# Attention steps on TensorE: the dense unit's hi and lo products around the turned weights, and exponentials ahead of the copy on ScalarE

## What is computed

```
p = h @ w_in[l]                                   # dense: GLU, q/k/v, gates
u = a * sigmoid(g); u = dwconv1d(u, dw, dw_b)     # convolution branch, 31 taps
u = silu(layernorm(u, ln_g, ln_b))
q, k = rope_2d(q), rope_2d(k)
s = concat([q . k_window + bias, q . k_context])  # 8 heads of 64
p = softmax(s)
out = p_window @ v_window + p_context @ v_context
y = sigmoid(gates) * (conv, attention branches)
```

## Time and profile before

| what | value |
|---|---|
| median of 3 runs | 3333.02 us (3327.91 to 3340.66) |
| profiled execution | 3339.16 us, span of the core 3336.9 us |
| PE, PEld busy | 87%, 71% |
| DVE, ACT, POOL busy | 53%, 37%, 46% |
| mean granted clock of TensorE | 0.932 of full |
| POOL `split_lo`, line 223 | 493 x 2482 ns |
| ACT `split_hi`, line 215 | 493 x 1054 ns |
| DVE taps, line 1834 | 234 x 1232 ns |

### The profile page before, as it was taken

How to read it: one execution, slowest core, us unless ns; L and a number is a source line. 1 busy time by engine, 2 the same in 40 slices (tenths; PEclk the granted TensorE clock), 3 DMA queues, 4 the chain that set the end, 5 groups by cost and what they waited for, 6 DMA issues and landing times.

```text
span 3336.9 us, 44321 instructions
## 1 busy us (share of the span) xinstructions
PE 2909.7 (87%) x15992; PEld 2353.6 (71%) x15992; DVE 1755.2 (53%) x2143; ACT 1234.8 (37%) x1781; POOL 1534.0 (46%) x773
## 2 busy tenths in 40 slices
PE   6988788999999775789789878999979887899997
PEld 6977434777777765689667666787767666677876
DVE  6866663352334556645478745423334985452424
ACT  4443222332233343454424432523332363243423
POOL 3442201333444585567477623444445773334443
PEclk9978899999999898899899998999989998999999
DMA  4302796222332322355332112222232221223221
GB/s 174 99 29 77 228 323 218 88 71 81 101 94 86 104 89 94 104 157 163 102 98 72 59 57 76 95 94 90 94 106 82 76 64 57 76 76 100 93 91 69
DMA packets 125811, 342.47 MB, mean 103 GB/s; under 512 B 37216, under 2 KB 45536, under 8 KB 125024
## 3 DMA queue, kind: packets, MB, share of 16 engines
q1 hardware_dynamic: 96800, 321.71, 29.7%
q10 hardware_dynamic: 28864, 18.76, 2.0%
HBM read 330.61 MB, written 7.45 MB: 101 GB/s over the span
## 4 chain that ended last, share of the span: by engine, by line
PE 57%; DVE 14%; POOL 7%; issue 6%; DVEq 5%; ACT 4%; DMA 3%; POOLq 2%; ACTq 1%; SPq 0%
PE ps L258 28%; PE ps L276 18%; POOL wlo L223 7%; DVE co L1834 4%; DVEq L1835 3%; DMA wraw<-w_ada 2%; PE ps L1942 2%; POOLq L1925 2%; DVE nacc L350 1%; ACT whi L215 1%; PE ps L565 1%; DVE sm L1810 1%; DVE mv L1996 1%; PE ps L1564 1%; DVE pex L1819 1%
## 5 line engine op out<-in xcount | busy, mean ns | idle before, releaser
L223 POOL TENSOR_TENSOR wlo<-wraw,whi 128x1024 fp32r<-128x1024 f32 x493 | 1216.2, 2482 | 1686.2 <-ACT whi L215 1685.4
L215 ACT ACTIVATE whi<-wraw 128x1024 fp32r<-128x1024 f32 x493 | 518.0, 1054 | 643.3 <-PE ps L276 286.9
L258 PE MATMUL ps<-xhi,whi 128*128 128x512 f32 (+2 forms) x1728 | 569.6, 352 | 8.9 <-DVE fa L2053 5.0
L258 PE MATMUL ps<-xlo,whi 128*128 128x512 f32 (+2 forms) x1728 | 565.1, 349 | 0.0
L258 PE MATMUL ps<-xhi,wlo 128*128 128x512 f32 (+2 forms) x1728 | 354.7, 349 | 5.9 <-POOL wlo L223 5.9
L258 PEld LDWEIGHTS ps<-xhi,whi 128*128 128x128 f32 x1728 | 318.8, 190 | 57.8 <-issue 7.5
L258 PEld LDWEIGHTS ps<-xlo,whi 128*128 128x128 f32 x1728 | 318.7, 190 | 44.9 <-issue 1.0
L258 PEld LDWEIGHTS ps<-xhi,wlo 128*128 128x128 f32 x1728 | 282.6, 189 | 50.2 <-POOL wlo L223 6.5
L1834 DVE SCALAR_TENSOR_TENSOR co<-ub,vec,co 128x512 f32<-128x512 f32 (+1 forms) x234 | 279.2, 1232 | 6.4 <-issue 0.9
L258 PE MATMUL ps<-hhi,whi 128*128 128x512 f32 (+1 forms) x616 | 223.1, 369 | 5.6 <-DVE gt L1993 3.3
L258 PE MATMUL ps<-hlo,whi 128*128 128x512 f32 (+1 forms) x616 | 222.4, 368 | 0.0
(11 more groups left out here) (322 smaller groups left out, 5016.6 us busy)
## 6 DMA issues: line engine op xcount, KB each, us to landing
wraw<-stream SPq DMA_DIRECT2D x493, 512.0 KB, 3.4
wraw<-w_ada SPq DMA_DIRECT2D x96, 512.0 KB, 5.6
biasb<-attn_bias ACTq DMA_DIRECT2D x32, 256.0 KB, 3.5
xin<-x0T SPq DMA_DIRECT2D x4, 528.0 KB, 6.3
s_u<-uk ACTq DMA_DIRECT2D x8, 264.0 KB, 2.9
res<-x0T ACTq DMA_DIRECT2D x1, 2048.0 KB, 8.7
s_y<-yk ACTq DMA_DIRECT2D x64, 32.0 KB, 4.0
yf<-s_y SPq DMA_DIRECT2D x8, 256.0 KB, 2.9
```

What stands on the lines that cost most here:

```text
L215: act.activation(whi[:, s], wraw[:, s], ACT.Copy).then_inc(hi_done[s], 1)
L223: pool.tensor_tensor(wlo[:, s], wraw[:, s], whi[:, s].bitcast(F32), ALU.subtract).then_inc(lo_done[s], 1)
L258: last = pe.matmul(ps[:, bank, 0:b - a], w[:, s, kt], x[:, kt, c0 + a:c0 + b], start=start, stop=stop)
```

## The change

In `mix_pe`, `pe_filler` is cut in two: `pe_filler_hi` issues the hi products, `pe_filler_lo` the lo products. In a step the turn of the step before stands between the hi and the lo products of the step's last unit; the values stand at the end of the step, behind the unit and its post product. Behind the last step of scores this holds too: the turn of step N - 1 stands between hi and lo of unit U+28, the values of step N - 2 behind U+28 and those of step N - 1 behind U+29. Before, turn and values stood right behind the scores, ahead of the units.

In `mix_act` the exponentials of the step stand ahead of the copy of the turned weights. The evacuation of the first unit of a step with two (c0) stands ahead of both; it stood behind them. `out_hi_act` stays behind the copy. The programs of VectorE, POOL and SyncE are the same.

```
--- before.py
+++ after.py
@@ -1553,7 +1553,7 @@
             return None
         return 3 * h + "qkv".index(k) if p.lat else h
 
-    def pe_filler(pe, p, g):
+    def pe_filler_hi(pe, p, g):
 
         s, rnd = slot(g)
         hi_split(pe, g, 0, 0)
@@ -1563,6 +1563,11 @@
         for kt in range(NT):
             pe.matmul(o, whi[:, s, kt], xhi[:, kt, 0:p.T], start=kt == 0, stop=False)
             pe.matmul(o, whi[:, s, kt], xlo[:, kt, 0:p.T], start=False, stop=False)
+
+    def pe_filler_lo(pe, p, g):
+
+        s = g % R
+        o = ps[:, s % 2, 0:p.T]
         lo_split(pe, g, 0, 0)
         for kt in range(NT):
             last = pe.matmul(o, wlo[:, s, kt], xhi[:, kt, 0:p.T], start=False, stop=kt == NT - 1)
@@ -1642,22 +1647,25 @@
         for g in range(p.U + 8, p.U + 8 + PRE):
             if g < p.U + 10:
                 all_freed(pe, g)
-            pe_filler(pe, p, g)
+            pe_filler_hi(pe, p, g)
+            pe_filler_lo(pe, p, g)
             if held:
                 pe_post(pe, p, held)
             held = g
         for n in range(p.N + 2):
             if n < p.N:
                 scores_pe(pe, p, n)
-            if 0 < n <= p.N:
-                turn_pe(pe, p, n - 1)
-            if n >= 2:
-                values_pe(pe, p, n - 2)
-            for g in fillers(p, n) if n < p.N else [p.U + 28 + n - p.N]:
-                pe_filler(pe, p, g)
+            units = fillers(p, n) if n < p.N else [p.U + 28 + n - p.N]
+            for g in units:
+                pe_filler_hi(pe, p, g)
+                if g == units[-1] and 0 < n <= p.N:
+                    turn_pe(pe, p, n - 1)
+                pe_filler_lo(pe, p, g)
                 if held:
                     pe_post(pe, p, held)
                 held = g
+            if n >= 2:
+                values_pe(pe, p, n - 2)
         all_freed(pe, p.U + 30)
         pe.wait_ge(p.o_v.sem, p.o_v.past("lo", 3))
         for g in range(p.U + 30, p.U + 36):
@@ -1736,17 +1744,15 @@
         for n in range(p.N + 2):
             for g in late:
                 evac_act(act, p, g)
+            now = fillers(p, n) if n < p.N else [p.U + 28 + n - p.N]
+            for g in now[:-1]:
+                evac_act(act, p, g)
+            if n < p.N:
+                exps_act(act, p, n)
             if 0 < n <= p.N:
                 copied_act(act, p, n - 1)
-            if n < p.N:
-                exps_act(act, p, n)
-                now = fillers(p, n)
-            else:
-                now = [p.U + 28 + n - p.N]
             if out_due(p, n) is not None:
                 out_hi_act(act, p, out_due(p, n))
-            for g in now[:-1]:
-                evac_act(act, p, g)
             late = now[-1:]
         for g in range(p.U + 29, p.U + 33):
             evac_act(act, p, g)
```

## The result

| | before | changed |
|---|---|---|
| median of 6 runs each | 3332.06 us | 3360.11 us |
| ratio, 95% interval | 1 | 1.0068 (1.0050 to 1.0086) |
| profiled execution: span | 3336.9 us | 3348.5 us |
| medians of a later series, 21 and 6 runs | 3334.44 us | 3354.29 us, 1.0061 (1.0036 to 1.0086) |

The changed kernel is slower by 20 to 28 us, outside the range of the prediction (3316 to 3349) and on the side that got 0.12.

What follows compares the result with a forecast made beforehand. VectorE's start on its last convolution taps, behind the last out_lo, was taken to end each stage. Loops at -2.5 us each in l0 and l1, ends +1.4, -0.4, +1.1, sum -2.9 from 3333.0: 3330 us, range 3316 to 3349.

Steps and rivals of the forecast that it cites:

- the side that got 0.12: Chance given to a result slower by more than the 16.7 us that a measurement can tell from no change.
- the end: Loop end to convolution mean: later last values, partly recovered by fewer taps beside GpSimd; +1.4 (c0), -0.4 (l0), +1.1 us (l1).
- the relief: Last taps behind the l0 loop: less time shared with GpSimd gives back 2.2 us, between 0 and 3.
- the open gate from step 10 on: Steps from 10: VectorE runs 4 us or more behind the scores, so the later turn delays no exponentials; no cost.
- the taps: Steps 10 to 14: later GpSimd splits free the fourth tap, 2.0 us in two of five steps; -4.0 us a pass.
- the term for steps 0 to 9: l0 and l1 loops: exponentials delayed by the later turn in steps 7 and 9; +1.5 us each, bounds 0 to 3.
- its values now stand behind a wait at the post: Aside on step 6, where TensorE no longer stalls at the turn; no cost of its own was given.
- The unit has three steps of slack, TensorE does not see it; so nothing for that: On ACT, evacuation, split_hi and thereby GpSimd's split_lo queue behind the later copy; counted as no cost.
- The rivals: Three alternatives: slower, 3344 us, chance 0.23; faster, taps free and TensorE bound, 3317, 0.2; no effect, 3333, 0.1.
- The slower one: VectorE paces all, shifted splits free no tap, ends come late without relief; +11.2 us, 3344 us, chance 0.23.
- its extension: Addition to the slower rival: splits fall on free two-tap groups in three steps a pass; 12 us more, 3356.
- A: Theory from the follow-up experiments, not the prediction: values lengthen the round VectorE, post, values, scores; 5 to 8 us a loop.

Runs made afterwards that it cites:

- e5: Kernel before with only ACT's order of the change (evacuations, exponentials, copy), TensorE's order as before: ratio 0.9991 to the kernel before.
- e13: e1 with one more wait on ACT: in steps with a post the copy of the turned weights also waits for that post; ratio 1.0028 to the kernel before.
- e14: e1 with the scores of steps 6, 7 and 9 computed twice in l0 and l1; ratio 1.0002 to the kernel before.
- e1: Changed kernel with the values product moved from behind the post product to in front of it; ratio 0.9998 to the kernel before.
- e4: Kernel before with the change made in pass c0 alone, l0 and l1 in the old order; ratio 1.0009 to the kernel before.
- e12: The changed kernel itself, run again with a second profile; median 3354.29 us.
- e6: Changed kernel with the values product moved to right behind the scores in all three passes; ratio 1.0010 to the kernel before.

## Why the prediction was wrong

**Right: what bounds the kernel.** TensorE waits 22.29, 13.12 and 13.51 us for `lmu`, and what moved the time moved VectorE's date. The waits at the turn went, as forecast: no row of them is left in the changed loop.

**Right: the end.** From the last scores to the mean l0 lost 0.1 us and l1 1.1; the forecast was -0.4 and +1.1. In c0 the last `out_lo` came 3.1 us later, counted from the first scores, where 3.1 was forecast, and the mean 2.1, where 1.4 was. How much of the 2.1 lies behind the last scores does not repeat: 0.5 in the first profile of the changed kernel, 1.8 in the second. In l0:

```profile
1902.38 1.06 DVE L1833 TENSOR_TENSOR hlo<-ps,hhi 128x512 fp32r<-128x512 f32 x1 [8.45 <-ACT hhi L1720]
1903.34 29.64 DVE L1840 SCALAR_TENSOR_TENSOR co<-ub,vec,co 128x512 f32<-128x512 f32 x26
```

The 26 last taps took 29.64 us for 31.05 in the earlier trace rows, 1.4 us of the relief that the prediction put at 2.2. A wrong sign: VectorE's wait ahead of `out_lo` in c0 was to grow by 3 us and fell from 8.66 to 5.98. The date was right, but VectorE came later to it too.

**Wrong: the open gate from step 10 on.** For these steps the sum has -4.0 us a pass, by the taps, and nothing for the gate; they grew by 2.1 us in l0 (53.98 to 56.13) and 2.6 in l1. That is about half of the miss: the loops were put at -2.5 us and came out at +10.3 and +8.9, and of these 12.8 and 11.4 us, 6.2 and 6.6 lie here. The taps themselves did what was forecast. VectorE's busy time in steps 10 to 15 fell by 3.7 in l0 and 3.8 in l1; two groups of four taps took 2.9 us. One of them, behind the exponentials of step 11, with the split after it and the copy in between, as described:

```profile
1845.50 2.90 DVE L1840 SCALAR_TENSOR_TENSOR co<-ub,vec,co 128x512 f32<-128x512 f32 x4
```

But in e5, with the same order on ACT and the turn in front, the busy time was 41.1 us: one group short at 2.9, and another of 6.1. The later turn belongs to the cause. And it takes as much as it gives: the scaling of the next step,

```profile
1855.82 0.17 DVE L1821 RECIPROCAL sm<-sm 128x2 f32<-128x2 f32 x1 [5.28 <-ACT pex L1714]
```

waited 5.28 us, for 1.52 before, for exponentials that stood behind the turn of 1851.93. In all, the waits for the exponentials in these steps grew from 11.3 to 15.9 us in l0 and from 11.3 to 16.3 in l1, more than the taps gave back; 3.8 and 0.8 of l0's growth lie in steps 12 and 13, the two whose taps had become shorter. `out_lo`, which had not waited, waited 1.3 and 1.4 us, by the copy's new place. So "From step 10 on ... the gate is open" is a step that failed. It took VectorE's lag behind the scores from the kernel before, and its own term for the taps shortens that lag: in step 12 the maxima were ready 5.97 us behind the start of the scores, for 8.07 before. Besides, the turn ended there 8.4 us behind that start and not 5.9. The scores had waited 5.25 us, and behind this idle time scores and hi ran slower:

```profile
1844.57 1.23 PE L1611 MATMUL ps<-kT,qT 64*128 64x256 f32 x4 [5.25 <-ACT pex L1714]
...
1851.93 1.03 PE L1621 MATMUL ps<-cst,pex 128*128 128x128 f32 x8
```

These 7.36 us (1851.93 - 1844.57) would be 4.89 by the earlier trace rows; the granted clock over them is 0.63 of full. Before, only scores and turn were run at that clock before the gate opened (the turn ended 3.04 us behind the start in that step); now hi stands ahead of the turn too.

**Wrong: the term for steps 0 to 9, which failed twice.** It stood at +1.5 us, for the exponentials of steps 7 and 9 (measured there: a wait of 0.7 us in step 7); these ten steps lost 8.2 in l0 and 6.4 in l1, which is the other half of the miss (6.7 and 4.9 us).
- In a parenthesis it says that "its values now stand behind a wait at the post", and counts nothing for it. That wait is for VectorE's work of the same step, and the next scores stand behind the values, so each such product is on VectorE's own round, and in steps 6 and 8, where TensorE idles 4.39 and 3.36 us before the post, the values take about twice their time. By e13 this is 4.0 and 3.9 us at most, of which VectorE's longer waits for scores show 3.2 and 2.0. The 4.39 us wait of TensorE with the 3.40 us wait of VectorE behind it is that round.
- It prices the copy's new place with "The unit has three steps of slack, TensorE does not see it; so nothing for that". TensorE doesn't see it, true; but VectorE does. The late copy puts GpSimd's splits on VectorE's work on q, k and v, and `out_hi` behind it makes `out_lo` wait inside the loop (3.4 us), which the prediction looked at only for the last head pair. By e13 it is 8.6 and 5.3 us, counted over the whole loop, and the changed kernel's copy is later still. The prediction had the rule for this in hand (the Trainium skill, "SBUF — State Buffer", section "Who interferes with whom": one of the two engines blocks for the other's whole instruction) and applied it only to the taps, where it paid, not to the other VectorE work in the same steps, where it cost. The rows of step 8 agree with the rule: 0.68 became 1.45, and 0.18 became 1.28, each reaching just past the end of GpSimd's instruction.

**The rivals.** The slower one gave 3344 (3356 with its extension) by late ends and splits on two-tap groups. With the extension its time was near the measured one, but by another way. None of the rivals had the round through the post or the late copy's splits on the work on q, k and v.

**Still open.** How large A is by itself: e14, the one run that puts work behind the post and leaves the copy where it was, came out at 2.7 and 0.1 us. And the part of c0, 2.1 us, which no run took apart. It was 2.1 to 2.6 us in the runs with c0 in the changed order or with one piece of it moved back (e1 to e4, e12 to e14), and 0.8 and 0.6 in e5 (turn and values in front) and e6 (values in front).

## What to carry to other kernels

When a product moves within a queue that one engine works off in order, ask what it now stands behind: a wait that was free because nothing urgent followed becomes part of a round as soon as something does. Write down the round of the engine that bounds the stage (here VectorE, post, scores, VectorE) and count every instruction on it at the clock that the engine has after idling. And a step of ACT or GpSimd with slack to its own reader can still cost, by where it makes another engine's work fall; count that for every instruction of the bounding engine in the new place, not only for those that gain. And where the sum has a term that makes the bounding engine earlier, look again at every gate that was open only because that engine was late.

## What the runs showed of the hardware

- A copy of VectorE with one SBUF input, 128x64 f32, took 1.28 us instead of 0.18, until GpSimd's 1.26 us instruction was over. All 326 such copies of q, k and v that began more than 0.05 us inside a GpSimd instruction were held to its end. It is not only instructions with two inputs that are held up. The Trainium skill, "SBUF — State Buffer", section "Who interferes with whom", says this of copies that use both ports; the trace agrees.
- Behind an idle time of 4.39 us, TensorE ran 5.7 us of work (post, values, scores) at a granted clock of 0.52, where the same pieces take 3.1. A wait of TensorE off the critical path can thus lengthen what is on it.
- Identical code ahead of the first attention step took from 1140.9 to 1160.4 us in different executions, as much as the effect studied. Sums by pass repeated within about 1 us in a second profile of the changed kernel; over kernels with the same order in a loop, the loop's length differed by up to 3.1 us.
